# A transformer step on one core: the scaling of attention probabilities is moved from VectorE to GpSimd, and VectorE's order around it is rewritten

## The reference, cut to what matters

```python
def gqa_block(qb, k, v):                     # 8 query heads, 2 key heads, head size 64
    s = jnp.einsum('bqhgd,bshd->bhgqs', qb, k).astype(jnp.float32) * (HEAD_DIM ** -0.5)
    p = jax.nn.softmax(s, axis=-1).astype(v.dtype)
    return jnp.einsum('bhgqs,bshd->bqhgd', p, v)

def diff_block(qb, k, v, lam):               # 4 heads, two maps of 64 each, values of 128
    s = jnp.einsum('bqhmd,bshmd->bhmqs', qb, k).astype(jnp.float32) * (HEAD_DIM ** -0.5)
    p = jax.nn.softmax(s, axis=-1)
    a = p[:, :, 0] - lam[None, :, None, None] * p[:, :, 1]
    return jnp.einsum('bhqs,bshe->bqhe', a.astype(v.dtype), v)
```

## Time and profile before

| | |
|---|---|
| median of 3 runs | 1146.9 us (1146.23 to 1149.08) |
| the profiled execution, its own time | 1145.81 us |
| its span | 1144.0 us |
| PE busy | 1097.6 us, 96% of the span |
| DVE busy | 528.1 us, 46% |
| ACT busy | 363.2 us, 32% |
| POOL busy | 132.4 us, 12% |
| mean granted TensorE clock | 0.992 of full |

### The profile page before, as it was taken

One profiled execution on the slowest core, in us unless ns is written; L12 is line 12 of the kernel. 1 busy time (PEld: TensorE's weight loads), 2 busy tenths in 40 slices (PEclk: granted clock), 3 DMA queues, 4 the chain that ended last, 5 costly groups with the idle time before them and its releaser, 6 DMA issues.

```text
span 1144.0 us, 28118 instructions
## 1 busy us (share of the span) xinstructions
PE 1097.6 (96%) x12524; PEld 828.2 (72%) x12524; DVE 528.1 (46%) x961; ACT 363.2 (32%) x846; POOL 132.4 (12%) x173
## 2 busy tenths in 40 slices
PE   6999999999999999999998999999999999999993
PEld 4679875666677777777877877777777777777761
DVE  4574538879958142334976033332233223333235
ACT  4333327778753223022163221222222222211103
POOL 2332300000000000002012111111110111110021
PEclk9999999999999999999999999999999999999997
DMA  9932242111031545359987999999999999999993
GB/s 359 299 107 68 77 84 63 35 31 41 1 109 38 184 147 147 106 190 300 355 303 320 402 398 406 407 405 409 414 406 405 408 404 408 405 408 405 410 321 143
DMA packets 86747, 295.32 MB, mean 258 GB/s; under 512 B 27249, under 2 KB 28530, under 8 KB 62050
## 3 DMA queue, kind: packets, MB, share of 16 engines
q1 hardware_dynamic: 79104, 269.77, 61.5%
q0 software_dynamic: 6528, 20.10, 6.1%
q10 hardware_dynamic: 994, 3.65, 0.9%
HBM read 273.25 MB, written 15.00 MB: 252 GB/s over the span
## 4 chain that ended last, share of the span: by engine, by line
PE 85%; DMA 7%; issue 2%; ACT 2%; DVE 2%; SPq 1%; POOLq 0%; POOL 0%; ACTq 0%; DVEq 0%
PE ps L1207 39%; PE ps L772 10%; PE ps L774 9%; PE ps L773 9%; PE ps L994 4%; PE ps L1013 3%; PE ps L1032 2%; PE ps L1036 2%; DMA x_dram<-y_row,rows_t 2%; DMA x_dram<-xn_p 1%; DMA raw_first<-in_w_in_dram 1%; DMA x_f<-x_dram 1%; PE ps L794 1%; DMA raw<-in_w_in_dram 1%; PE ps L978 1%
## 5 line engine op out<-in xcount | busy, mean ns | idle before, releaser
L2124 DVE SCALAR_TENSOR_TENSOR y_row<-ps,gates,gate_q 32x256 f32<-32x256 f32 (+1 forms) x184 | 88.3, 480 | 238.5 <-PE ps L1207 236.0
L1564 ACT ACTIVATE h_t<-ps 128x256 f32<-128x256 f32 x48 | 15.0, 384 | 374.7 <-PE ps L1207 374.7
L772 PE MATMUL ps<-w_hi,ht 128*128 128x512 f32 (+1 forms) x320 | 124.2, 388 | 0.6 <-DVE q_n L1728 0.6
L774 PE MATMUL ps<-w_hi,ht 128*128 128x512 f32 (+1 forms) x320 | 121.8, 381 | 0.0
L773 PE MATMUL ps<-raw_lo,ht 128*128 128x512 f32 (+1 forms) x320 | 121.7, 380 | 0.0
L1207 PE MATMUL ps<-late,xe 128*32 128x256 f32 x1824 | 103.6, 379 | 0.0
L537 DVE TENSOR_TENSOR raw_lo<-raw,w_hi 128x1024 fp32r<-128x1024 f32 x48 | 58.2, 1234 | 78.9 <-ACT w_hi L532 78.2
L1207 PEld LDWEIGHTS ps<-late,xe 128*32 128x32 f32 x1824 | 77.0, 110 | 23.3
L1207 PE MATMUL ps<-raw,xe 128*32 128x256 f32 x1392 | 88.1, 379 | 0.9 <-issue 0.8
L532 ACT ACTIVATE w_hi<-raw 128x1024 fp32r<-128x1024 f32 x48 | 48.7, 1053 | 123.6 <-DMA raw<-in_w_in_dram 68.1
L2354 POOL DMA_INDIRECT xg<-x_dram,rows x48 | 46.1, 961 | 320.7 <-PE ps L1207 293.2
(11 more groups left out here) (315 smaller groups left out, 1831.0 us busy)
## 6 DMA issues: line engine op xcount, KB each, us to landing
late<-in_w_exp_down_dram SPq DMA_DIRECT2D x25, 1024.0 KB, 20.4
late<-in_w_exp_up_dram SPq DMA_DIRECT2D x21, 1024.0 KB, 28.8
late<-in_w_exp_gate_dram SPq DMA_DIRECT2D x17, 1024.0 KB, 24.7
raw<-in_w_in_dram SPq DMA_DIRECT2D x16, 1024.0 KB, 5.5
raw<-in_w_exp_gate_dram SPq DMA_DIRECT2D x16, 1024.0 KB
raw_gate<-in_w_exp_up_dram SPq DMA_DIRECT2D x14, 1024.0 KB
raw<-in_w_exp_up_dram SPq DMA_DIRECT2D x13, 1024.0 KB
raw_gate<-in_w_exp_down_dram SPq DMA_DIRECT2D x13, 1024.0 KB
```

The source lines that it names most:

```text
L772: pe.matmul(b, stat_hi(k, tt), hi[:, kk, :], start=first, stop=False)
L774: mm = pe.matmul(b, stat_lo(k, tt), hi[:, kk, :], start=False, stop=last)
L2124: return dve.scalar_tensor_tensor(y_row[n % 2][32 * v:32 * v + count, 256 * q:256 * q + 256], bank(b, o, o + 256, src), gates[src, n % EG, ...
```

## The change

POOL now multiplies both maps of the plain units, and the second map of the differential units, each with an instruction that takes two scalars per row: the reciprocal and either a column of ones or lambda. DVE keeps the reciprocals, which now signal POOL (`s_inv`), and the subtraction of the differential units, which now waits for POOL (`s_second`) and stands between the two row maxima. PE waits for POOL in plain units.

```diff
                     else:
-                        pe.wait_ge(s_nrm, 2 * i + tiles[-1] // per + 1)
+                        pe.wait_ge(s_nrm, i + 1)
+                        if tiles[-1] >= per:
+                            pe.wait_ge(s_second, i + 1)
...
             def inverse_sums(i):
                 o = 2 * i % 8
                 dve.wait_ge(s_exp, 2 * i + 2)
-                dve.reciprocal(row_inv[:, o:o + 2], row_sum[:, o:o + 2]).then_inc(s_dve, 1)
-                own()
-
-            def normalise(i):
+                dve.reciprocal(row_inv[:, o:o + 2], row_sum[:, o:o + 2]).then_inc(s_inv, 1)
+
+            def combine(i):
...
-                dve.wait_ge(s_dve, own(0))
-                if p < PLAIN:
-                    dve.tensor_scalar(a, a, row_inv[:, o:o + 1], None, ALU.mult).then_inc(s_nrm, 1)
-                    dve.tensor_scalar(b, b, row_inv[:, o + 1:o + 2], None, ALU.mult).then_inc(s_nrm, 1)
-                else:
-                    g = 2 * HB + p - PLAIN
-                    dve.tensor_scalar(b, b, row_inv[:, o + 1:o + 2], lam[:, g:g + 1], ALU.mult, ALU.mult)\
-                       .then_inc(s_c1, 1)
-                    dve.wait_ge(s_c1, i - PLAIN * NT + 1)
+                if p >= PLAIN:
+                    dve.wait_ge(s_second, i + 1)
                     dve.scalar_tensor_tensor(a, a, row_inv[:, o:o + 1], b, ALU.mult, ALU.subtract).then_inc(s_comb, 1)
...
                 if 1 <= i <= len(PUS):
                     inverse_sums(i - 1)
-                    normalise(i - 1)
                 if 0 <= i - LAG < len(PUS) and i not in QUERY_SLOTS:
                     probs_turned(i - LAG)
                 if i + 1 < len(PUS):
                     row_max(2 * i + 2)
+                if 1 <= i <= len(PUS):
+                    combine(i - 1)
+                if i + 1 < len(PUS):
                     row_max(2 * i + 3)
...
+            for i, (p, t) in enumerate(PUS):
+                cols, o = KTL * P if t < NTL else P, 2 * i % 8
+                a, b = prob_row(2 * i)[:, 0:cols], prob_row(2 * i + 1)[:, 0:cols]
+                g = 2 * HB + p - PLAIN
+                pool.wait_ge(s_inv, i + 1)
+                if p < PLAIN:
+                    pool.tensor_scalar(a, a, row_inv[:, o:o + 1], one, ALU.mult, ALU.mult).then_inc(s_nrm, 1)
+                    pool.tensor_scalar(b, b, row_inv[:, o + 1:o + 2], one, ALU.mult, ALU.mult).then_inc(s_second, 1)
+                else:
+                    pool.tensor_scalar(b, b, row_inv[:, o + 1:o + 2], lam[:, g:g + 1], ALU.mult, ALU.mult)\
+                        .then_inc(s_second, 1)
```

More of the change, by code:

```diff
@@ L427, in build @@
         s_sc = sem("s_sc"); s_max = sem("s_max"); s_exp = sem("s_exp");
-        s_nrm = sem("s_nrm"); s_c1 = sem("s_c1"); s_comb = sem("s_comb"); s_ptr = sem("s_ptr")
+        s_nrm = sem("s_nrm"); s_inv = sem("s_inv"); s_second = sem("s_second"); s_comb = sem("s_comb"); s_ptr = sem("s_ptr")
         s_ph = sem("s_ph"); s_pl = sem("s_pl"); s_pv = sem("s_pv"); s_oev = sem("s_oev");
```

## The result

| | before | after |
|---|---|---|
| median | 1146.9 us (7 runs, 1146.1 to 1149.08) | 1152.02 us (7 runs, 1151.54 to 1154.74) |
| ratio | | 1.0047, interval 1.0037 to 1.0056 |
| the profiled execution, its span | 1145.81, 1144.0 us | 1152.75, 1150.9 us |

The change costs 5.1 us. The forecast was 1153.7 us, 1.7 above the median.

A forecast was written before the change was run, and what follows sets the result against it. PE was taken to bound attention. Plain half 0 plus differential half 4 x 1.69 = 6.8 us on the 1146.9 us median gave 1153.7 us; range 1147.8 to 1162 us, the forecast's own 1151 to 1157.

The forecast's parts named there:

- The bound: Attention stage: PE is busy nearly throughout, 82.22 of 83 and 68.71 of 69 us, so time taken from DVE is worth nothing.
- The plain half at 0: Plain units: POOL's two scalings, 2.4 us a unit of about 4, fit before PE's transposes, so they cost 0.
- My limit of 1.5 us a scaling: Plain half: POOL's delivery to the transposes fits up to about 1.5 us an instruction; at 1.61 it misses by some 0.3.
- The wait of scores B in the second slot: Second differential slot of each pair: PE's scores B wait 0.51 us for the exponential behind the delayed maximum B.
- maximum B 1.80 us behind maximum A: Sign in the second differential slot: with the subtraction between them, maximum B starts 1.8 us behind maximum A.
- the context slot's transposes behind the subtraction: End of each differential pair: transposes wait for reciprocal, POOL and subtraction until 18.0 us; next pair's scores start at 18.66.
- 4 x 1.69 = 6.8 us: Differential half: each of four pairs takes 18.66 instead of 16.97 us, losing 1.69, 6.8 in all.
- POOL's price: One scaling of 768 columns on POOL was taken at 1.2 us, the middle between 0.81 and 1.61.
- The lower bound of POOL's price: At 0.81 us a scaling, a differential pair loses 1.30 us, 5.2 in all.
- Hidden: Rival: only the second slot's 0.51 us is left of each differential pair, 2.0 us in all, 1148.9; chance 0.22.
- Faster: Rival: DVE's shorter queue removes today's waits in both halves, up to 3.6 us, 1143.3; chance 0.05.
- POOL slow: Rival: POOL at 2.0 us or more a scaling bounds the plain half; 1166 at 2.4; chance 0.15 including hold-up by DVE.

The follow-up runs named there:

- experiment one: The changed kernel with POOL scaling only plain units; differential units as before, DVE scaling B and subtracting ahead of both maxima: 1147.04 us.
- eight: Against the kernel before: reciprocal one slot earlier, between the maxima; DVE does all scalings and subtracts behind both maxima, POOL nothing: 1146.85 us.
- Experiment four: Against the changed kernel: POOL still scales, but DVE takes each reciprocal one slot earlier, between the maxima, and subtracts behind both: 1147.11 us.
- experiment six: The changed kernel with a second POOL pass over both maps in the plain units: 1159.95 us.
- experiment seven: The changed kernel with POOL's plain-unit scalings using one scalar instead of two, without the column of ones: 1162.27 us.
- experiment five: The changed kernel with a second POOL pass over B, by ones, in the differential units: 1163.15 us.

## Why the prediction was right

**The bound.** PE was the bound, and time taken from DVE was worth nothing by itself. Experiments one and eight show it from both sides.

**The plain half at 0.** Right, by experiment one. Maxima and copies run beside POOL at their old length. Their groups after, on DVE:

```profile
L1803 DVE TENSOR_REDUCE neg_max<-ps 128x1 f32<-128x768 f32 x64 | 59.5, 953 | 53.4 <-PE ps L994 53.4
...
L1828 DVE COPY p_t<-ps 128x512 f32<-128x512 f32 x16 | 11.0, 689 | 18.1 <-PE ps L1015 18.1
```

The same groups took 953 and 688 ns in the kernel before. Taken alone, the 34 maxima of the plain stretch, where POOL is busy for 35 of 83 us, lie between 945 and 959 ns; before, 35 lay between 947 and 959. The Trainium skill, page "SBUF — State Buffer", section "Who interferes with whom", has it that a VectorE instruction with at most one SBUF input outside the two-port modes does not contend with GpSimd; these rows agree. Whether the subtraction, which reads two, would contend is not shown: POOL's scaling never ran beside it, in any of the runs. My limit of 1.5 us a scaling wasn't tried between 0.98 and a doubled one; the doubled one is beyond it.

**The differential half.** The places were right. The wait of scores B in the second slot, maximum B 1.80 us behind maximum A (268.88 and 270.68), and the context slot's transposes behind the subtraction are all there. The first is smaller than forecast. I wanted it at some 0.5 us; the profile names 0.17 of idle time, and scores B start 0.34 us later than PE would have had them (272.71 against 271.63 + 0.745). The slots of one pair, in us (after, from the timeline, where scores start at 267.92, 271.63, 275.70, 279.67, 283.67 and 286.45):

| | 1 | 2 | 3 | 4 | context | pair |
|---|---|---|---|---|---|---|
| before | 3.64 | 3.64 | 3.97 | 3.81 | 1.91 | 16.97 |
| forecast | 3.64 | 4.15 | 3.97 | 3.99 | 2.91 | 18.66 |
| after | 3.71 | 4.07 | 3.97 | 4.00 | 2.78 | 18.53 |

**The term that was mis-sized** is "4 x 1.69 = 6.8 us". It measured 0.97 + 1.56 + 1.57 + 1.09 = 5.2. Two errors are in it. The larger is the factor of four: I took every pair as the one in the earlier trace rows. During the first pair's scores PE still works off the last plain units, whose slots are longer, and behind the fourth pair's context scores there is no next pair to be late for. These two lost 0.72 and 0.60 us less than a pair was said to. That the neighbours are the reason is read from the order of the work; no run isolates it. The smaller is POOL's price, 1.2 us against 0.98. It lies on the path once a pair, so it is worth -0.22; in its place the six transposes behind the wait took 0.81 us until the next scores (285.64 to 286.45) instead of 0.66, +0.15. The two nearly cancel, so a full pair came out only 0.13 us under its forecast.

**The lower bound of POOL's price** gave 5.2 us, which looks like the result, but it is so by two wrong steps: at 0.81 us a pair should have lost 1.30, and it lost 1.56.

**The rivals.** *Hidden* had PE feel only the second slot, and its 1148.9 is under the lowest run; the context slot adds 0.87 us a pair (2.78 against 1.91). *Faster* needed DVE's shorter queue to take existing waits away. Experiment four took the subtraction out of the maxima's way and still gained nothing in the median; by its timeline the context slot's wait is ACT's. *POOL slow* did not occur with this form. Experiments six and seven show what it would have been: the limit I named for the plain half was real, and the form without the second scalar is beyond it. There it was the stall and not POOL's busy time: in experiment seven a plain pair has 8 x 2.21 + 2 x 0.61 = 18.9 us of POOL's work and takes 21.56, with one wait of PE of 1.39 us. The half clock at the stage's start was not in my sum.

**Not settled.** Why the one-scalar form is slower on POOL was not looked into. Experiments five to seven changed POOL's time and, through the waits, PE's clock together; no run held the clock still, and what makes it fall is not settled either (see the last section). No run tested what holds the context slot in experiment four.

## What to carry to other kernels

Relieving an engine pays only where the chain of waits passes through it; before moving work, ask which instruction behind it somebody waits for. When two products are needed by two consumers (here maximum A and maximum B, each with its exponential and its PSUM bank behind it), an instruction put between them delays the second by its full length. The repair was free: put the work that is wanted later behind both, and what feeds it (here the reciprocal) early enough that its product is there in time. When a term is multiplied by a count, look at the first and the last of the count, whose neighbours differ.

## What the runs showed of the hardware

- On POOL, a scaling of 128x768 float32 takes 0.98 us with two scalars and 2.21 us with one (128 columns: 0.45 and 0.61). The Trainium skill, page "GPSIMD Engine Reference", section "3.1 Elementwise — side-by-side cycle accounting", says that for up to two operations the loop is bound by the port, at 1.03 cycles an element. At the 1.2 GHz that the section counts with, I estimate 0.86 ns a column from that figure. The two-scalar form's 0.83 ns is near it; the one-scalar form, with one operation fewer, takes 2.5 ns, three times as much, and the measurement decides.
- The same scalings on VectorE took 0.62 us with one scalar and 0.68 with two (L1817, L1821, 128x768). What is cheap there says nothing of which form is cheap on POOL.
- In the changed kernel PE's single waits in the differential half are at most 0.4 us, and the granted clock stays at 1.00. Waits of 1.30 and 1.34 us in experiments five and six were followed by about 3 and nearly 7 us at 0.50, in which the same eight matmuls took 2.78 and 2.86 instead of 1.56 us. A wait on the bounding engine can cost more than its length.
- Not every such wait did this. In experiment seven one of 1.39 us comes once a plain pair (until 213.80, 235.37 and 256.94), and the clock stays at 1.00 around each. These stood alone. Where the clock fell in the attention stage, PE had waited twice in a short time: 0.60 and 1.30 us in experiment five, 1.34 and 0.52 us in experiment six, 1.57 and 0.65 us in experiment seven. What decides was not tested.
